# Attention rounds with scores and values between a block's tiles, pool blocks last, and half the first layer's modulation blocks in the state-space stage

## What is computed

```
def layer(x, cvec, p, ctx):
    sh1, sc1, g1, sh2, sc2, g2 = modulation(cvec, p['w_mod'], p['b_mod'])   # silu(c) @ w_mod + b_mod
    h = rmsnorm(x, p['norm1_g']) * (1.0 + sc1) + sh1
    pool_u, q, k, v, z, xbc, dt_raw, gate_logits = in_projection(h, p['w_in'])
    pool_out = pool_mixer(pool_u, ...)          # windowed means, 4 groups, a 128x128 product each
    attn_out = windowed attention(q, k, v)      # 8 query heads, 2 key heads, a sink logit
    ssd_out  = ssd_mixer(z, conv(xbc), dt_raw)  # depthwise convolution of 5, silu, state-space scan both ways
    merged = (g_pool * (pool_out @ w_pool_o) + g_attn * (attn_out @ w_attn_o) + g_ssd * (ssd_out @ w_ssd_o))
    x = x + g1 * (merged @ w_out)
    h = rmsnorm(x, p['norm2_g']) * (1.0 + sc2) + sh2
    x = x + g2 * (square(relu(h @ w_mlp1)) @ w_mlp2)
```

## Time and profile before

| what | us |
|---|---|
| median of 3 runs | 1506.45 (1504.0 to 1508.64) |
| the profiled execution, its own time | 1502.93 |
| its span in the profile | 1501.1 |
| TensorE busy | 1450.3 (97%) |
| VectorE busy | 878.7 (59%) |
| ScalarE busy | 678.0 (45%) |
| GpSimd busy | 113.8 (8%) |

### The profile page before, as it was taken

How to read it: one execution, slowest core, us unless ns; L and a number is a source line. 1 busy time by engine, 2 the same in 40 slices (tenths; PEclk the granted TensorE clock), 3 DMA queues, 4 the chain that set the end, 5 groups by cost and what they waited for, 6 DMA issues and landing times.

```text
span 1501.1 us, 20942 instructions
## 1 busy us (share of the span) xinstructions
PE 1450.3 (97%) x8335; PEld 1324.0 (88%) x8335; DVE 878.7 (59%) x1423; ACT 678.0 (45%) x1180; POOL 113.8 (8%) x107
## 2 busy tenths in 40 slices
PE   6899999999999999999998999999999999999998
PEld 2799778788899899999987997887889999999998
DVE  2686545765466645455546876567745666555563
ACT  3855543433544524242428566443435454334351
POOL 0002000430001000000010030032300010000000
PEclk9999999999999999999999999999999999999999
DMA  9556653132434665655646442223343434444441
GB/s 321 178 183 200 210 170 112 54 115 84 140 113 143 191 199 171 212 181 174 221 130 183 123 116 71 85 72 97 84 113 112 127 118 123 125 127 126 127 127 42
DMA packets 187334, 210.25 MB, mean 140 GB/s; under 512 B 10798, under 2 KB 156006, under 8 KB 187238
## 3 DMA queue, kind: packets, MB, share of 16 engines
q1 hardware_dynamic: 187238, 208.93, 45.3%
HBM read 204.97 MB, written 3.93 MB: 139 GB/s over the span
## 4 chain that ended last, share of the span: by engine, by line
PE 86%; DVE 7%; ACT 4%; issue 2%; DMA 1%; SPq 0%; ACTq 0%; DVEq 0%
PE bank L647 22%; PE bank L648 22%; PE bank L649 22%; PE bank L661 3%; PE bank L662 3%; PE bank L663 3%; DVE tb L1545 2%; PE bank L679 1%; PE seg_ps L679 1%; PE y_ps L892 1%; PE y_ps L915 1%; PE seg_ps L779 1%; PE y_ps L795 1%; DVE wlo L1462 1%; PE y_ps L805 1%
## 5 line engine op out<-in xcount | busy, mean ns | idle before, releaser
L1462 DVE TENSOR_TENSOR wlo<-raw,whi 128x1024 fp32r<-128x1024 f32 (+1 forms) x288 | 352.6, 1231 | 246.1 <-ACT whi L1053 245.0
L1053 ACT CAST whi<-raw 128x1024 fp32r<-128x1024 f32 (+1 forms) x288 | 297.1, 1037 | 326.9 <-PE bank L649 176.8
L647 PE MATMUL bank<-ahi,whi 128*128 128x384 f32 (+1 forms) x1280 | 443.0, 346 | 0.0
L648 PE MATMUL bank<-alo,whi 128*128 128x384 f32 (+1 forms) x1280 | 433.6, 339 | 0.0
L649 PE MATMUL bank<-ahi,wlo 128*128 128x384 f32 (+1 forms) x1280 | 433.2, 338 | 0.0
L647 PE MATMUL bank<-bhi,whi 128*128 128x384 f32 x768 | 262.4, 342 | 0.9 <-ACT arena_s L1105 0.9
L648 PE MATMUL bank<-blo,whi 128*128 128x384 f32 x768 | 259.4, 338 | 0.0
L649 PE MATMUL bank<-bhi,wlo 128*128 128x384 f32 x768 | 259.4, 338 | 0.0
L647 PEld LDWEIGHTS bank<-ahi,whi 128*128 128x128 f32 x1280 | 241.6, 189 | 14.5 <-issue 13.1
L648 PEld LDWEIGHTS bank<-alo,whi 128*128 128x128 f32 x1280 | 241.7, 189 | 3.9 <-issue 3.3
L649 PEld LDWEIGHTS bank<-ahi,wlo 128*128 128x128 f32 x1280 | 241.7, 189 | 0.0
(11 more groups left out here) (232 smaller groups left out, 1389.4 us busy)
## 6 DMA issues: line engine op xcount, KB each, us to landing
raw<-in_w_mlp_dram SPq DMA_DIRECT2D x128, 512.0 KB, 3.7
raw<-in_w_in_dram SPq DMA_DIRECT2D x104, 512.0 KB, 3.8
raw<-in_w_mod_dram SPq DMA_DIRECT2D x96, 512.0 KB, 6.1
raw<-in_w_ssd_o_dram SPq DMA_DIRECT2D x16, 512.0 KB, 3.5
raw<-in_w_out_dram SPq DMA_DIRECT2D x16, 512.0 KB, 3.5
raw<-in_w_pool_o_dram SPq DMA_DIRECT2D x8, 512.0 KB, 3.8
raw<-in_w_attn_o_dram SPq DMA_DIRECT2D x8, 512.0 KB, 3.5
raw<-in_w_in_dram SPq DMA_DIRECT2D x8, 256.0 KB, 3.3
```

Of the source, the lines that this page charges most:

```text
L647: nc.tensor.matmul(dst, uh[:, k, tm_cols(m)], hi[k0 + k], start=first and k == 0, stop=False)
L648: nc.tensor.matmul(dst, uh[:, k, tm_cols(m)], lo[k0 + k], start=False, stop=False)
L1053: nc.scalar.copy(dst, src).then_inc(hi_ready, 1)
L1462: nc.vector.tensor_tensor(rest, full, top.bitcast(F32), ALU.subtract).then_inc(lo_ready, 1)
```

## The change

Five things move; no work is added or dropped, apart from four loads of ScalarE's function tables.

1. **Within a round** the filler unit is split: after its tile m = 0 TensorE does the value product of the round before and the scores of the next (`half_way`). ScalarE and VectorE take the value result one round later, in the same place of their own order. The value product of round 11 stands behind the twelve sums of the handover, its copy and rest behind what the sums need; the scan's first output waits for it (`ydiag`).
2. **Pool units 2 and 3** stand behind xbc 11, not behind xbc 3. The silu of the last convolution pair, before in round 1, comes right behind its convolution; `pooled(2)` and `pooled(3)` move to rounds 1 and 3.
3. **Modulation units** of the first layer: sixteen stay at the same positions in stage 2 (behind pool 1, xbc 5, xbc 9, pool 3). The other sixteen leave the rounds and stand in fours behind fillers 13, 17, 20 and 25, in the state-space stage.
4. **Row and columns** of that sum are made in block z. The row has a place of its own (`modrows`), and the wait for the columns stands behind gsb.
5. **Bank 3** stays with the sum until z 4, before until the second poa unit.

```diff
-IN_ORDER = [("xbc", 0), ("xbc", 1), ("pool", 0), ("pool", 1), ("xbc", 2), ("xbc", 3), ("pool", 2), ("pool", 3)]
-IN_ORDER += [("xbc", i) for i in range(4, 12)]
+IN_ORDER = [("xbc", 0), ("xbc", 1), ("pool", 0), ("pool", 1)] + [("xbc", i) for i in range(2, 12)] + [("pool", 2), ("pool", 3)]
-FIRST_MOD2 = {("pool", 1): range(0, 4), ("pool", 3): range(4, 8), ("xbc", 7): range(8, 12), ("xbc", 11): range(12, 16),
-              **{("round", i): range(16 + 2 * i, 18 + 2 * i) for i in range(8)}}
+FIRST_MOD2 = {("pool", 1): range(0, 4), ("xbc", 5): range(4, 8), ("xbc", 9): range(8, 12), ("pool", 3): range(12, 16),
+              ("fill", 13): range(16, 20), ("fill", 17): range(20, 24), ("fill", 20): range(24, 28),
+              ("fill", 25): range(28, 32)}
...
-        if (l, name, i) == (0, "poa", 1):
+        if (l, name, i) == (0, "z", 4):
             free = (0, 1, 2, 3)
...
                         ins.then_inc(gemm_step, 1)
+                        if m == 0 and between:
+                            between()
...
+                def half_way(i):
+
+                    if i >= 1:
+                        pv(i - 1)
+                    if i < 11:
+                        scores(i + 1)
...
                 for i in range(12):
-                    fill()
+                    fill(between=lambda: half_way(i))
                     prob_transposes(i)
-                    if i < 11:
-                        scores(i + 1)
-                    first_mod2("round", i)
                     if 0 <= i - MIX_ROUND < 4:
                         pool_mix(i - MIX_ROUND)
-                    pv(i)
-                    if l == 0 and i == 9:
-                        mod_columns(0, 1)
-
-
-                pe.wait_ge(modc_ready, l * 2 + 2)
...
                 ins.then_inc(acsT_done, 1)
+                pv(11)
...
                     seg(g, 0)
+                    first_mod2("fill", (13, 20)[g])
                     pe.wait_ge(state_loaded, (l * 2 + g + 1) * 32)
                     transposes4(1, stage[:, 1])
...
                     fill(slot[5])
+                    first_mod2("fill", (17, 25)[g])
                     pe.wait_ge(stT_ready, (l * 2 + g) * 2 + 2)
                     transposes4(8, stage[:, 0])
...
                 for i in range(8):
                     gemm_tm("z", i, 512)
+                    if l == 0 and i == 3:
+                        pe.wait_ge(aux_free, 26)
+                        mod_columns(0, 1)
...
                     qk_copies({3: (0, 1), 4: (2, 3), 5: (4,)}.get(b, ()))
-                    if b < 2:
-                        pool_in(b)
-                    if b < 5:
-                        conv_out(b)
+                    if b == 0:
+                        pool_in(0)
+                    conv_out(b)
                     if b == 2:
                         kdup_rows()
+
+                pool_in(1)
...
                 ahead("xbc", 11)
-                conv((10,))
+                conv((10, 11))
+                ahead("pool", 3)
                 fill()
                 head_max(0)
                 for i in range(12):
...
                     if i < 11:
                         head_max(i + 1)
+                    if i:
+                        attn_rest(i - 1)
                     if 0 <= i - MIX_ROUND < 4:
                         pool_rest(i - MIX_ROUND)
-                    attn_rest(i)
-                    if i == 0:
-                        conv((11,))
-                        pooled(3)
+                    if i == 1 or i == 3:
+                        pooled(2 + i // 2)
                     if i >= 7:
                         fill()
-                    if l == 0 and i == 10:
-                        modulation(0, 1)
                     if i == 10:
                         slot_columns()
```

More of the change, by code:

```diff
@@ L85, in unit_order @@
         out.append(fill[0])
-        for i in range(12):
-            out.append(fill[i + 1])
-            out += [(0, "mod2", n) for n in FIRST_MOD2.get(("round", i), ()) if l == 0]
-        out += fill[13:]
+        for n, u in enumerate(fill[1:], 1):
+            out += [u] + [(0, "mod2", m) for m in FIRST_MOD2.get(("fill", n), ()) if l == 0]
         out += run(l, "z", 8) + run(l, "gsb", 4) + run(l, "so", 8) + run(l, "wo", 8)
@@ L307, in backbone_step @@
         crow = arena_s[0:16, 0:P]
-        modrow = arena_s[:, 4096 + 4 * PPW:4096 + 4 * PPW + 512]
+        modrows = {(0, 1): arena_s[:, 3072:3584]}
+        for at in ((0, 0), (1, 0), (1, 1)):
+            modrows[at] = arena_s[:, 4096 + 4 * PPW:4096 + 4 * PPW + 512]
         gate = [arena_g[:, k * T:(k + 1) * T] for k in range(4)]
@@ L555, in _ @@
                     load(name, i)
-                    first_mod2("round", r - 1)
                     if r == 0:
@@ L560, in _ @@
                         sp.dma_start(new_v_r[l * P:l * P + P, :], val[:, 0, :]).then_inc(kv_out, 16)
+                fills = [(name, i) for name, n in POOL_FILL + SSD_FILL for i in range(n)]
                 for name, n in SSD_FILL:
@@ L638, in halves, with gemm_cm @@
                     return whi[:, SPLIT_AT[u] % WS, :], wlo[u % RAW]
-                def gemm_cm(name, i, hi, lo, k0, first, last, cols=T):
+                def gemm_cm(name, i, hi, lo, k0, first, last, cols=T, between=None):
                     uh, ul = (w.rearrange("p (k n) -> p k n", k=4) for w in halves(UNIT[l, name, i]))
@@ L819, in _, with fill @@
                 filled = [0]
-                def fill(n=1):
+                def fill(n=1, between=None):
                     for _ in range(n):
@@ L825, in fill @@
                         if name in GATES:
-                            gemm_cm(name, i, ahi, alo, 4 * (i % 2), i % 2 == 0, i % 2 == 1)
+                            gemm_cm(name, i, ahi, alo, 4 * (i % 2), i % 2 == 0, i % 2 == 1, between=between)
                             continue
@@ L888, in ydiag @@
                     pe.wait_ge(w_ready, (l * 2 + g) * 3 + t + 1)
+                    if t == 0 and g == 0:
+                        pe.wait_ge(attn_ready, l * 12 + 12)
                     if t or g:
@@ L1279, in fill @@
                         ahead(name, i)
+                        if between:
+                            between()
                         if name in GATES and i % 2 == 1:
@@ L1286, in _ @@
                     n = 1 if PAIRS[i][0] == 0 else 3
-                    fill()
+                    fill(between=(lambda: attn_round(i - 1)) if i else None)
                     act.wait_ge(pT_done, l * 12 + i + 1)
@@ L1360, in _ @@
                     ahead("z", 4 * n + 3)
+                    if l == 0 and n == 0:
+                        mod_rows(0, 1)
                     for t in range(TT):
@@ L1630, in _ @@
                     modulation(l, 1)
-                ahead("pool", 3)
                 def head_max(i):
@@ L1824, in _ @@
                             .then_inc(yz_ready, 1)
+                    if l == 0 and n == 0:
+                        modulation(0, 1)
                 ahead("gsb", 1)
```

20 lines of the change are left out of this document (10 added, 10 removed).

## The result

The changed kernel takes **1485.81 us** (median of four runs, 1485.38 to 1486.33), the kernel before 1507.43 beside it (1504.0 to 1508.64): a ratio of 0.987, with a 95% interval of 0.9852 to 0.9888. The profiled execution of the changed kernel took 1486.14 us with a span of 1484.3. Against the profiled execution before, 16.8 us went; the medians differ by 21.6. So two things need an explanation: 5.2 us more between the two traces than the forecast sum of 11.6, and 4.8 us by which the medians differ and the two traces don't. On another chip (x7_after) the changed kernel took 1488.04 us, 16.7 less than the kernel before beside it.

A forecast was written before the change was run, and what follows sets the result against it. TensorE, busy for 97% of the span, bounds the kernel. Rounds 7.7 + modulation units 0.5 + 2.2 + clock 3.2 - pool blocks 2.0 = 11.6 us gained, 1506.45 to about 1495; range 1491 to 1499, eight times in ten 1488 to 1503.

The forecast's parts named there:

- Term (c): Rounds: unit's first product behind plain fp32 work costs more; eight rounds without masks have one more change each, 0.9 us lost.
- Waits of the rounds: Both layers' rounds: TensorE's waits at probability transposes, value products and a bank lose their cause, 11.2 us gained.
- (a) Second scores: Second scores come sooner and wait for the first exponentials: 0.3 us in layer 0, 1.1 in layer 1.
- (b) The loop: Loop through three engines closes each round, 6.4 us against 6.2: rounds 1 and 2 lose 1.2 us in both layers.
- Modulation units: Layer 0: grouping sixteen units in fours gains 0.5 us; filling TensorE's waits in the state-space stage gains 2.2.
- Clock: Layer 0's handover: low clock, mean 0.88 over 28 us, goes with the waits; 3.2 us back, between 0 and 3.4.
- Pool blocks last: Input projection: convolution chain loses the pool blocks it rested on; 1.0 us lost per layer, 2.0 together, between 0 and 5.
- The slower rival: Rounds: the loop through the engines becomes the bound and the kernel slower, 1512 at 0.7 us a round; chance 0.07.

The follow-up runs named there:

- x1_old_rounds: Changed kernel with the old order of the rounds put back, pool blocks last and modulation units moved as changed: 1497.18 us, ratio 0.9948.
- y3_pool_only: Kernel before with only the pool blocks last and the convolution's last silu ahead of the rounds: 1500.58 us, ratio 0.9976.
- x3_old_mod: Changed kernel with the sixteen modulation units put back in layer 0's rounds: 1503.27 us, ratio 0.9997.
- z3_both: Changed kernel with VectorE's rest of the values ahead of the next maxima and group 0's states loaded earlier on SyncE: 1482.63 us, ratio 0.9856.
- the 67 runs: Runs of the unchanged kernel before, in four groups, comparing time with mean clock: correlation -0.83; 1502.2 us at 0.993, 1508.5 at 0.987.
- x4_before: The kernel before, unchanged, run and profiled once more: 1505.0 us, profiled execution 1505.07 us.
- x2_old_pool: Changed kernel with the pool blocks, and the convolution's last silu in round 1, put back: 1494.38 us, ratio 0.9925.

## Why the prediction was right or wrong, point by point

- **The time fell below the range for two reasons of like size.** Term (c) was 4.0 us off, and 4.8 us more came in the medians, most likely by the clock. Either alone would have left 1490 to 1491; both together make 1486.
- **Waits of the rounds: right in size, wrong in cause.** 11.2 us were to go and 2.6 to come (a and b), 8.6 net; measured 8.5. The prediction names the silu that leaves round 1 among the reasons, but books all 11.2 on the rounds and only a loss on the pool blocks. x1_old_rounds shows that about half of the idle time, and two thirds of the wait at the transposes, goes without the new order; y3_pool_only shows that wait going from 8.9 to 3.9 us with the pool blocks last; x3_old_mod shows that the new order needs the units away.
- **(a) Second scores:** 0.3 and 1.1 us forecast, 0.37 and 0.81 measured, behind the subtraction named; moving it took away half of layer 1's.
- **(b) The loop:** 1.2 us forecast in rounds 1 and 2; waits of 1.8 us came, in rounds 2 and 4, at the rest of the values. The order on VectorE was the cause, and costs nothing to change. In z3_both, where it is changed, the rounds of both layers take 3.9 us less in all: ahead of late transposes the last product of a unit takes 0.33 us to the next start for 0.18, and the list of waits doesn't count this.
- **(c) Changes between kinds: the step that failed.** "the eight rounds without have one more each: 8 x 0.11 = 0.9" lost, and nothing for the rounds with masks; measured 3.1 gained, 4.0 us off. I counted changes of type and looked at one pair alone, the first product of a unit. Start to start, the last transpose takes 0.20 us ahead of scores and 0.03 ahead of a unit, a pool product 0.31 ahead of values and 0.03 ahead of a unit. Part of it comes back at the unit's first product (0.26 us behind transposes, 0.28 behind values, 0.37 behind a pool product, for 0.175 inside a unit), which is why the units' row grew by 2.3 to 2.5 us a layer while the other rows shrank by more. A round without masks, in the kernel before, then in the changed one, layer 1:

```profile
969.85 0.38 PE L795 MATMUL y_ps<-cst,arena_s 128*128 128x128 f32 x2
970.16 0.49 PE L779 MATMUL seg_ps<-arena_s 64*128 64x128 f32 x4
970.69 0.44 PE L805 MATMUL y_ps<-arena_s,arena_g 128*64 128x128 f32 x4
...
975.64 0.44 PE L795 MATMUL y_ps<-cst,arena_s 128*128 128x128 f32 x2
```
```profile
962.67 0.38 PE L798 MATMUL y_ps<-cst,arena_s 128*128 128x128 f32 x2
...
965.10 0.44 PE L808 MATMUL y_ps<-arena_s,arena_g 128*64 128x128 f32 x4
965.47 0.49 PE L782 MATMUL seg_ps<-arena_s 64*128 64x128 f32 x4
...
968.11 0.38 PE L798 MATMUL y_ps<-cst,arena_s 128*128 128x128 f32 x2
```

  A round took 5.79 us, 0.24 of it a wait, and takes 5.44: 0.11 less work, where the forecast had 0.11 more. If the eight such rounds are alike, 1.8 of the 4.0 us lie in them, and the rest in the rounds with masks, which the prediction put at nothing. That the 3.1 us are the order's and not shorter waits is shown by x1_old_rounds, with half the idle time and the same 91.8 us of work. Why a pair costs what it does stays open.
- **Modulation units:** 0.5 forecast and measured. In the state-space stages 2.2 forecast and measured, but differently: layer 0 gained 1.6, because a wait of 1.3 us for loaded states came up that I had not priced ("the stage has room": by bandwidth it had, but the store before the load stood behind weight loads), and layer 1 gained 0.6, as in every kernel with the new rounds.
- **Clock:** 3.2 forecast, 3.0 measured between the two traces. What failed is the last step: taking the profiled execution as 3.5 us better than the median and shifting the forecast by the same 3.5. By the 67 runs most of such a difference goes with the mean clock, and x4_before shows one more low stretch in a slower execution; so the medians gained up to 4.8 us more on the first chip, by this account clock as well. No profile of an execution at the median was taken there, so this is likely and not shown.
- **Pool blocks last:** 2.0 lost forecast, 1.5 measured, at the places named. That the move gains 3.6 us on the whole was hidden in the first term.
- **Start of the program:** 0.95 us of the difference between the traces is chance, and in no term.
- **The slower rival** (the loop becomes the bound): x2_old_pool and x3_old_mod show such waits, 6.5 and 8.9 us at the transposes. Neither kernel is slower than the one before, but most or all of the gain was one part of the change away.

## What to carry to other kernels

Before moving small work to shorten a loop over several engines, ask what stands ahead of each of its steps on the other engines' queues: a late weight load cost nothing until the loop's copy stood behind it. Parts of such a change can be worth 0.1 to 0.3% each alone and 1.1 to 1.3% together, and two of them together nothing, so test them in pairs before dropping one. Where the clock falls behind waits, a profile at the best clock hides part of what removing the waits brings: compare the clock over many runs first.

## What was unexpected of the hardware

- Useless products in the place of four waits made the kernel 0.23% faster; its mean clock rose from 0.9906 to 0.9934.
- A wait of 1.65 and one of 0.46 us with small work between them were followed by a stretch at the lower level (x4_before, 992 to 995), and in another execution of the same program they were not.
- What a product costs from start to start depends on its follower: 0.03 or 0.31 us for the same pool product, 0.03 or 0.20 for the same transpose. The follower's own step changes too, so only the sum over a round tells what an order is worth.
